# Low parts of every fourth weight block move from VectorE to GpSimd, and three unsplit blocks are split

## What is computed

```python
# first block: modulation, one wide projection, two attentions, gated merge
mod = silu(c) @ w_ada + b_ada                      # 2048 x 6144
h = rms_norm(x, g_pre) * (1 + scale) + shift
proj = h @ w_in                                    # 2048 x 20032
a = mla_branch(...) * silu(z_mla);  bb = dilated_branch(...) * silu(z_dil)
merged = sigmoid(gl_mla) * (a @ w_mla_proj) + sigmoid(gl_dil) * (bb @ w_dil_proj)
x = x + gate * rms_norm(merged @ w_o, g_post)
# second block, layer 0: indexer top-k attention; layer 1: stick-breaking attention
x = layer_norm(ALPHA * x + y, g, b)                # y = mixer(x), twice
x = x + (p @ w_ple) * sigmoid(x @ w_ple_gate)
```

## Time and profile before

| | us |
|---|---|
| median of 3 runs | 2376.17 (2375.61 to 2376.22) |
| profiled execution | 2375.65, of it the span 2374.3 |
| TensorE busy | 2351.3 (99%) |
| VectorE busy | 1464.9 (62%) |
| ScalarE busy | 1140.7 (48%) |
| GpSimd busy | 87.2 (4%) |
| chain that ended last: TensorE / VectorE / ScalarE / DMA | 90% / 5% / 2% / 2% |
| HBM traffic | 201 GB/s over the span, about 400 in the first 120 us |

### The profile page before, as it was taken

How to read it: one execution, slowest core, us unless ns; L and a number is a source line. 1 busy time by engine, 2 the same in 40 slices (tenths; PEclk the granted TensorE clock), 3 DMA queues, 4 the chain that set the end, 5 groups by cost and what they waited for, 6 DMA issues and landing times.

```text
span 2374.3 us, 28762 instructions
## 1 busy us (share of the span) xinstructions
PE 2351.3 (99%) x11224; PEld 1965.6 (83%) x11224; DVE 1464.9 (62%) x1997; ACT 1140.7 (48%) x1471; POOL 87.2 (4%) x121
## 2 busy tenths in 40 slices
PE   9999999999999999999999999999999999999999
PEld 5688898988889988888888888888788788888777
DVE  7887765554555455686756675566765555456675
ACT  4344454544445554443444445554545555455453
POOL 0000100000000000000000100000200000000020
PEclk9999999999999999999999999999999999999999
DMA  9986643555554457887655555455665555555565
GB/s 397 401 298 207 196 148 115 173 178 188 188 165 146 139 186 253 288 291 241 213 195 191 181 174 162 163 165 185 223 213 188 169 177 167 185 161 177 187 221 177
DMA packets 131241, 478.98 MB, mean 202 GB/s; under 512 B 15281, under 2 KB 15537, under 8 KB 125985
## 3 DMA queue, kind: packets, MB, share of 16 engines
q1 hardware_dynamic: 126080, 458.41, 58.4%
q0 software_dynamic: 3728, 17.76, 2.1%
q10 hardware_dynamic: 1298, 0.97, 0.1%
HBM read 470.80 MB, written 6.29 MB: 201 GB/s over the span
## 4 chain that ended last, share of the span: by engine, by line
PE 90%; DVE 5%; ACT 2%; DMA 2%; issue 1%; SPq 0%; POOL 0%; ACTq 0%; DVEq 0%; POOLq 0%
PE G L841 25%; PE G L843 25%; PE G L842 25%; PE A L852 4%; DMA ada<-in_weights 2%; DVE wlo L1472 2%; PE A L841 2%; PE A L843 2%; PE A L842 2%; PE A L923 1%; PE A L903 1%; PE G L837 1%; ACT whi L1128 1%; PE A L996 1%; DVE CP L1780 1%
## 5 line engine op out<-in xcount | busy, mean ns | idle before, releaser
L1472 DVE TENSOR_TENSOR wlo<-raw,whi 128x1024 fp32r<-128x1024 f32 (+3 forms) x781 | 922.9, 1185 | 698.2 <-ACT whi L1128 695.9
L1128 ACT ACTIVATE whi<-raw 128x1024 fp32r<-128x1024 f32 (+3 forms) x781 | 800.0, 1025 | 832.3 <-PE G L843 744.5
L841 PE MATMUL G<-whi,XH 128*128 128x512 f32 (+3 forms) x2804 | 1082.1, 386 | 9.1 <-DVE wlo L1472 6.8
L843 PE MATMUL G<-whi,XL 128*128 128x512 f32 (+3 forms) x2804 | 1066.7, 380 | 0.0
L842 PE MATMUL G<-wlo,XH 128*128 128x512 f32 (+3 forms) x2804 | 1065.7, 380 | 0.0
L841 PEld LDWEIGHTS G<-whi,XH 128*128 128x128 f32 x2804 | 526.7, 188 | 105.2 <-DVE wlo L1472 12.7
L843 PEld LDWEIGHTS G<-whi,XL 128*128 128x128 f32 x2804 | 526.3, 188 | 95.1
L842 PEld LDWEIGHTS G<-wlo,XH 128*128 128x128 f32 x2804 | 526.9, 188 | 90.2 <-issue 0.2
L841 PE MATMUL A<-whi,XH 128*128 128x512 f32 x192 | 77.2, 402 | 3.0 <-DVE wlo L1472 3.0
L1486 DVE CUSTOM_DVE_ANT_0 ada<-ada,dil 128x2048 f32<-128x2048 f32 x32 | 75.1, 2347 | 5.0 <-DMA ada<-in_weights 4.9
L842 PE MATMUL A<-wlo,XH 128*128 128x512 f32 x192 | 74.7, 389 | 0.0
(11 more groups left out here) (230 smaller groups left out, 1551.1 us busy)
## 6 DMA issues: line engine op xcount, KB each, us to landing
raw<-in_weights SPq DMA_DIRECT2D x724, 512.0 KB, 3.6
ada<-in_weights SPq DMA_DIRECT2D x32, 1024.0 KB, 11.2
raw<-in_weights SPq DMA_DIRECT2D x80, 384.0 KB, 3.1
raw<-in_weights SPq DMA_DIRECT2D x16, 288.0 KB, 2.9
spill<-nat POOLq DMA_DIRECT2D x8, 512.0 KB, 5.4
CP<-spill POOLq DMA_DIRECT2D x8, 512.0 KB, 6.5
raw<-in_weights SPq DMA_DIRECT2D x8, 336.0 KB, 3.2
FT<-in_xT SPq DMA_DIRECT2D x4, 512.0 KB, 5.7
```

What stands on the lines that cost most here:

```text
L841: pe.matmul(acc, xh[:, k, half], wh, start=(k == start), stop=False)
L843: ins = pe.matmul(acc, xl[:, k, half], wh, start=False, stop=(k == end - 1))
L1128: ac.activation(whi[r % NSPL][:, 0:2 * cols], raw[o.home[n]][:, 0:2 * cols], ACT.Copy).then_inc(hi_done, 1)
L1472: ve.tensor_tensor(wlo[r % NSPL][:, 0:2 * cols], raw[o.home[n]][:, 0:2 * cols], whi[r % NSPL][:, 0:2 * cols].bitcast(F32), ALU.subtract).t ...
```

## The change

Three blocks that were whole, 18, 21 and 27, are split like the rest. And for every block s with s % 4 == 2 from 18 on, but for three stretches around the norms (430 to 441, 566 to 579, 762 to 775), the subtraction that makes the low part is issued on GpSimd and no longer on VectorE: 185 blocks. It stands in GpSimd's stream at the place of the take in the common walk, ahead of the pieces of side work that follow it there. Since low parts are now finished by two engines, there are two counters, lo_done and lo_gp, and o.low gives the count to wait for; TensorE and SP wait for the one that belongs to the block.

```diff
-WHOLE = frozenset([*range(OPENING), 6, 9, 12, 15, 18, 21, 27])
+WHOLE = frozenset([*range(OPENING), 6, 9, 12, 15])
+
+GP_LOW = frozenset([s for s in range(18, 800) if s % 4 == 2 and not any(a <= s < b for a, b in ((430, 442), (566, 580), (762, 776)))])
...
+        self.low = {s: sum(x not in self.whole and (x in GP_LOW) == (s in GP_LOW) for x in range(s + 1))
+                    for s in range(len(self.slots))}
...
             else:
-                pe.wait_ge(lo_done, o.rank[s] + 1)
+                pe.wait_ge(lo_gp if s in GP_LOW else lo_done, o.low[s])
...
                 r = o.rank[o.slot_of[n]]
+                if o.slot_of[n] in GP_LOW:
+                    return
                 ve.wait_ge(hi_done, r + 1)
...
+        def take(n):
+            kind, w, c0, cols, k = plan[n]
+            if kind == "w" and o.slot_of[n] in GP_LOW:
+                r = o.rank[o.slot_of[n]]
+                gp.wait_ge(hi_done, r + 1)
+                gp.tensor_tensor(wlo[r % NSPL][:, 0:2 * cols], raw[o.home[n]][:, 0:2 * cols],
+                                 whi[r % NSPL][:, 0:2 * cols].bitcast(F32), ALU.subtract).then_inc(lo_gp, 1)
+
...
-                gp.wait_ge(lo_done, o.rank[65] + 1)
+                gp.wait_ge(lo_done, max(o.low[s] for s in range(66) if s not in o.whole and s not in GP_LOW))
...
         for kind, a, b in o.walk:
-            if kind == "move":
+            if kind == "take":
+                take(a)
+            elif kind == "move":
                 move(a)
...
                 else:
-                    sp.wait_ge(lo_done, o.rank[s] + 1)
+                    sp.wait_ge(lo_gp if s in GP_LOW else lo_done, o.low[s])
```

More of the change, by code:

```diff
@@ L642, in first_and_second_block @@
     moved = [sem(f"moved_G{n}") for n in range(4)] + [sem(f"moved_A{n}") for n in range(4)]
-    hi_done, lo_done, modulated, gated = (sem(n) for n in ("hi_done", "lo_done", "modulated", "gated"))
+    hi_done, lo_done, lo_gp, modulated, gated = (sem(n) for n in ("hi_done", "lo_done", "lo_gp", "modulated", "gated"))
     x_hi, x_lo, side_hi, rows_made, rows_gp = (sem(n) for n in ("x_hi", "x_lo", "side_hi", "rows_made", "rows_gp"))
```

## The result

The changed kernel takes 2405.5 us (median of 4 runs, 2402.0 to 2408.9) against 2376.2 (2375.6 to 2376.8): ratio 1.0119, 95% interval 1.0106 to 1.0131. The change costs 29 us, 1.2%; the forecast was 18.5 us, so its sum is 11 short, and the result lies on the upper edge of its range (2405). The profiled execution took 2405.38, its span 2404.1.

A forecast was written before the change was run, and what follows sets the result against it. TensorE, busy 99% of the span, bounds the kernel. Early 2, late places 9.1, ropes 3.8, tail 3.3 and small ones 0.3 sum to 18.5 us; 2375.65 + 18.5 = 2394 us, range 2379 to 2405.

The forecast's parts named there:

- The sign and the place: Whole kernel: slower (chance 0.81); nothing gained in undisturbed stretches, loss where VectorE's low part is already last.
- five late places: Blocks 445, 453, 469, 541, 743: low parts later by 1.8, 1.2, 2.3, 2.2 and 1.2 us.
- The price of a take: GpSimd's low part: 2.5 us for 128x1024, 1.9 for 768 wide; bounds 1.4 and 3.3.
- rival A: All GpSimd low parts cost 1.4 us, so waits after block 50 shrink: faster, 2370 us; chance 0.10.
- C: Rival: each GpSimd low part costs 3.3 us, so ropes, holds and tail lose more: 2412 us; chance 0.13.
- The lock: Shared ports: GpSimd's low part holds off VectorE operations with two SBUF operands up to 2.35 us, taking away 1.15.
- rival B: VectorE and GpSimd share the ports over long streams without locking each other out: 2381 us; chance 0.15.
- Early: Blocks 18 to 33: the splits' 2.1 us lost again and 1.1 to 3.4 more; +2, bounds -2 and +5.
- Ropes: Ten ropes: cosine products behind GpSimd's low part, seven late by 0.45 us and three by 0.2: +3.8.
- Tail: Blocks 778, 786, 794: GpSimd low parts behind reads of spilled rows, +1.9, +0.7 and +0.7 us: +3.3.
- Small ones: Blocks 114 and 458 lose 0.7 us through late high parts, block 94's wait of 0.4 goes: +0.3.
- The clock: TensorE's granted clock behind standstills: the prediction had no term and no size for it.

The follow-up runs named there:

- experiment 3: Changed kernel with eleven GpSimd low parts at late places given back to VectorE, 174 staying: 2391.3 us, ratio 1.0065.
- experiment 9: Changed kernel with GpSimd's order as in experiment 5 and no GpSimd low parts below block 74 or at late places, 159 of 185 staying: 2376.9 us, ratio 0.9999.
- experiment 6: Kernel before, with two idle SBUF-reading products on GpSimd at each place of a take, all low parts on VectorE: 2417.3 us, ratio 1.0169.
- experiment 7: Against experiment 6, GpSimd makes four zero fills, which read nothing, instead of the two idle products: 2381.2 us, ratio 1.0020.
- experiment 11: Changed kernel with GpSimd low parts only at blocks 52, 646, 678 and 710, and blocks 18, 21, 27 whole: 2373.6 us, ratio 0.9986.
- experiment 2: Changed kernel with blocks 18, 21 and 27 whole as before, the other GpSimd low parts staying: 2406.6 us, ratio 1.0121.
- experiment 1: Changed kernel with no low part on GpSimd, only blocks 18, 21 and 27 split: 2376.4 us, ratio 0.9999.
- experiment 4: Changed kernel with each GpSimd low part issued later, behind the ropes' cosine products, and the second layer's spilled-row reads behind them: 2411.8 us, ratio 1.0147.
- experiment 5: Against experiment 4, the spilled-row reads of both layers, six in all, stand behind the GpSimd low parts: 2396.4 us, ratio 1.0082.

## Why the prediction was right, and where it fell short

**The sign and the place.** Right: nothing is gained where TensorE doesn't wait, and the loss is made where VectorE's low part was already last. Experiment 3 gives back 14 us for eleven takes, experiment 9 all of it. The five late places were worked out to 0.25 us each; the net of 642, 674 and 706 was put at a loss of 0.4 and is a gain of 0.1.

**The price of a take.** Right: 2.45 for 2.5. So rival A falls (it needed 1.5). By its time alone, 2405.5, the run lies nearer to C (2412) than to my sum (2394); it is the 2447 ns of the row that decides, and C falls for this change, though experiment 6 shows about what it would have done: ropes and clock both grow.

**The lock.** Right: rival B falls by experiments 6 and 7, which hold GpSimd at the same places with and without reads, for 3.1 and 2.1 us: +40 and +4 us, and VectorE's low parts 1307 and 1226 ns. The step that left it open, reductions and sums beside GpSimd, is now seen both ways (experiment 11). The rule was drawn too narrowly, though: it is not only steps with two SBUF operands that are held. This one has a single one, beside the take that begins at 166.96, and takes 0.31 us otherwise:

```profile
167.04 2.48 DVE L1912 TENSOR_SCALAR dil<-dil 128x288 f32<-128x288 f32 x1
```

A copy within SBUF (L1884, 128x64, at 1349.61) is held in the same way, 2.44 us instead of 0.18. Neither makes a step in the block starts.

**Early.** The size came out right (2.1 for 2), the place wrong. My walk along VectorE's order had low part 33 at 125.7, if GpSimd gets the ports first, and that came true in the kernels in which it still stood as walked (experiments 2 and 3). In the changed kernel low parts 23 and 25 were late before that, at 93.38 and behind the take of 26 at 99.07. And the 2 us of the splits were no gain in the first place: experiment 1 has them eaten by VectorE without any take. That the size fits is in part luck: with small changes around it the same stretch cost 3.8 us in experiment 2, without the gain of the splits, and 3.0 and 1.8 of half clock in experiment 3.

**Ropes.** The term was mis-sized: 0.69 each for six of them and 1.05 for a seventh in this profile, and 0.48 for three, in place of 0.45 and 0.2. I had put VectorE's last two steps, 0.4 us, behind GpSimd's products. In fact six stand there, because the sine products of the second half queue behind the first half's sum, which waits for the cosine:

```profile
494.80 0.47 DVE L1656 TENSOR_TENSOR nat<-ra,rb 128x64 f32<-128x64 f32 x1 [4.55 <-POOL ra L2077]
495.19 0.21 DVE L1657 TENSOR_TENSOR nat<-ra,rb 128x64 f32<-128x64 f32 x1
495.32 0.21 DVE L1652 TENSOR_TENSOR rb<-nat,sinT 128x64 f32<-128x64 f32 x1
495.46 0.21 DVE L1653 TENSOR_TENSOR rb<-nat,sinT 128x64 f32<-128x64 f32 x1
495.77 0.23 DVE L1656 TENSOR_TENSOR nat<-ra,rb 128x64 f32<-128x64 f32 x1
495.91 0.22 DVE L1657 TENSOR_TENSOR nat<-ra,rb 128x64 f32<-128x64 f32 x1
```

That is 1.33 us from the first to the last, while only one cosine product, and not two, stands ahead of them.

**Tail.** 2.1 + 0.6 + 0.6 for 1.9 + 0.7 + 0.7, and 0.14 lost again behind each. The mechanism is the forecast one: with the reads behind the takes these steps are gone (experiments 4 and 5).

**Small ones.** 390 was missed: a product on VectorE (L1933, 128x512, two SBUF operands) took 2.56 us behind the take that began at 1152.15. Block 94 was taken for a gain of 0.4 and lost 0.8, since its rope is held as the others are.

**The clock.** The step that failed outright is one that isn't in the sum: the clock was taken as granted in full, because it was full throughout in the profile before. That profile was one execution. The kernel before has a standstill of 1.79 us itself, ahead of block 745, with the full clock behind it there; in the profiles of six of the other twelve kernels the half clock stands behind the same wait. The change adds three longer ones with the half clock behind them in this profile, waits of 1.95, 3.38 and 2.46 us. The four together are 6.3 of the 11 us that the forecast is short of. The other 4.7 are waits and order that came to 23.2 us in place of 18.5, ropes above all (2.8).

## What to carry to other kernels

An engine that takes work from another at the same ports does not relieve it while both have work: price the hold (here 2.35 us for 1.15 taken away), and look for the places where the relieved engine's result is already last. Count the order on the receiving engine as well: a product that was ready when called stands behind a 2.4 us step now, and everything queued behind its consumer moves with it. Where a forecast makes TensorE stand for some 2 us and more at a time, add the clock to it (here 1.5 to 1.7 us for each standstill) as a cost that comes in some executions and not in others. And one profile with the clock in full doesn't show that it stays so.

## What the runs showed of the hardware

The half clock behind a standstill was not expected: 1.5 to 1.7 us each (once 2.9), behind 7 of 16 made on purpose, and more often the longer they were; the same wait of 1.95 us had it in one execution and not in another, and that of 1.79 us ahead of block 745 in six profiles of thirteen. In experiment 4 it lasted twice as long at two places and cost 2.5 and 2.8 us. The spread of the runs, 2402 to 2409 for the changed kernel against 2375.6 to 2376.8 before, fits it, but only the profiled run of a kernel shows where the clock fell: the longest run of the change has the lowest mean clock (0.995, the others 0.997), and the kernel before itself was seen up to 2379.3 with a mean clock of 0.998 when many runs of it were made.

GpSimd's subtraction with two operands in SBUF costs 2.35 to 2.40 us for 128x1024 when nothing is in its way, 1.85 for 128x768. It waits for a VectorE reduction of two operands that is under way (2.99 us in experiment 11), and where it was seen waiting as one ended it got in ahead of VectorE's next low part (3.38 us instead of 1.23 in experiment 3, 3.39 in the changed kernel). VectorE operations seen held by it in the changed kernel: subtractions, sums and products of two SBUF operands, scans and the fused forms with two such operands, and also a copy and a TENSOR_SCALAR step with a single one (2.44 us instead of 0.18, 2.48 instead of 0.31). Not held: sums with one operand in PSUM (six of kept<-A,kept that began beside a take took 681 ns on the average, the others 680), copies out of PSUM (691 and 692) and reductions of one operand (943 both ways).
